# A two-layer hybrid trunk on one core: late mixer steps cut in two on TensorE, with modulation chunks between the pieces

## The reference

```python
mods = (jax.nn.silu(c) @ ada_w + ada_b).reshape(B, 3, 3, 1, D_MODEL)
x = residual(x, 0, _swiglu(modulate(x, 0), ffn_wg[0], ffn_wu[0], ffn_wd[0]), 0.5)
proj = modulate(x, 1) @ w_in
p_rw, p_gla, p_ml = _split(proj, [RW_PROJ, GLA_PROJ, ML_PROJ])
o_rw, ... = _rwkv7_mix(p_rw, ...)      # first mixer
o_gla, ... = _gla_mix(p_gla, ...)      # second: gated linear attention, gates from log_sigmoid(gdown @ a2 + a_b)
o_ml, ... = _mlstm_mix(p_ml, ...)      # third: mLSTM
mix = jnp.concatenate([o_rw, o_gla, o_ml], axis=-1) @ w_out
x = residual(x, 1, mix, 1.0)
x = residual(x, 2, _swiglu(modulate(x, 2), ffn_wg[1], ffn_wu[1], ffn_wd[1]), 0.5)
```

## Time and profile before

| | us |
|---|---|
| device time, median of 3 runs | 1668.06 |
| lowest, highest of them | 1665.26, 1680.5 |
| the profiled execution, its own time | 1668.73 |
| its span, first to last instruction | 1666.6 |

### The profile page before, as it was taken

One profiled execution on the slowest core, in us unless ns is written; L12 is line 12 of the kernel. 1 busy time (PEld: TensorE's weight loads), 2 busy tenths in 40 slices (PEclk: granted clock), 3 DMA queues, 4 the chain that ended last, 5 costly groups with the idle time before them and its releaser, 6 DMA issues. The chain is left out here.

```text
span 1666.6 us, 32873 instructions
## 1 busy us (share of the span) xinstructions
PE 1602.4 (96%) x14052; PEld 1472.9 (88%) x14052; DVE 930.4 (56%) x1593; ACT 672.4 (40%) x997; POOL 203.1 (12%) x271
## 2 busy tenths in 40 slices
PE   5999999999999999999999999999999989899997
PEld 2999999998777779999989999989977768899996
DVE  1544545587663675555474545465865456655544
ACT  2333344564323344333353333355532244543333
POOL 1000011100222330000210000110022242100011
PEclk9999999999997799999999999999999669999998
DMA  8765555443443173444645544734313325344441
GB/s 309 277 220 209 176 213 180 148 123 120 158 160 105 47 277 136 146 149 152 253 165 202 208 168 154 252 123 165 111 61 119 119 79 181 118 148 146 142 161 69
DMA packets 103864, 268.57 MB, mean 161 GB/s; under 512 B 39560, under 2 KB 42024, under 8 KB 103464
## 3 DMA queue, kind: packets, MB, share of 16 engines
q1 hardware_dynamic: 99304, 263.86, 46.1%
q10 hardware_dynamic: 4416, 2.62, 0.6%
HBM read 260.19 MB, written 6.26 MB: 160 GB/s over the span
## 5 line engine op out<-in xcount | busy, mean ns | idle before, releaser
L2408 DVE TENSOR_TENSOR wlo<-raw,whi 128x1024 fp32r<-128x1024 f32 x300 | 367.9, 1229 | 312.7 <-ACT whi L2256 310.0
L2256 ACT ACTIVATE whi<-raw 128x1024 fp32r<-128x1024 f32 x300 | 316.2, 1055 | 290.8 <-PE psV L2067 260.4
L2065 PE MATMUL psA<-XH,whi 128*128 128x320 f32 x1104 | 342.8, 311 | 2.7 <-DVE wlo L2408 2.4
L2066 PE MATMUL psA<-XL,whi 128*128 128x320 f32 x1104 | 341.4, 309 | 0.0
L2067 PE MATMUL psA<-XH,wlo 128*128 128x320 f32 x1104 | 341.3, 309 | 0.0
L2065 PE MATMUL psV<-XH,whi 128*128 128x320 f32 x848 | 266.5, 314 | 0.1
L2066 PE MATMUL psV<-XL,whi 128*128 128x320 f32 x848 | 262.9, 310 | 0.0
L2067 PE MATMUL psV<-XH,wlo 128*128 128x320 f32 x848 | 262.8, 310 | 0.0
L2065 PEld LDWEIGHTS psA<-XH,whi 128*128 128x128 f32 x1104 | 207.7, 188 | 5.1 <-issue 4.1
L2066 PEld LDWEIGHTS psA<-XL,whi 128*128 128x128 f32 x1104 | 207.6, 188 | 0.2
L2065 PE MATMUL psV<-HH,whi 128*128 128x320 f32 x672 | 207.6, 309 | 0.0
(11 more groups left out here) (413 smaller groups left out, 2005.2 us busy)
## 6 DMA issues: line engine op xcount, KB each, us to landing
raw<-weights_dram SPq DMA_DIRECT2D x402, 512.0 KB, 3.3
own<-weights_dram SPq DMA_DIRECT2D x56, 512.0 KB, 5.9
in_xh<-weights_dram SPq DMA_DIRECT2D x6, 512.0 KB, 4.2
in_xl<-weights_dram SPq DMA_DIRECT2D x6, 512.0 KB, 4.5
raw<-weights_dram SPq DMA_DIRECT2D x6, 384.0 KB, 3.6
raw<-weights_dram SPq DMA_DIRECT2D x8, 256.0 KB, 3.6
ZS<-st_rw_dram SPq DMA_DIRECT2D x2, 768.0 KB, 4.4
S<-st_gla_dram ACTq DMA_DIRECT2D x2, 768.0 KB, 4.8
```

Of the source, the lines that this page charges most:

```text
L2065: mm(out, split_hi(n)[:, k], hi[:, kt], start=first, stop=False)
L2066: mm(out, split_hi(n)[:, k], lo[:, kt], start=False, stop=False)
L2256: activation(split_hi(n), buffer(DENSE[n]), ACT.Copy).then_inc(hi_done, 1)
L2408: tt(split_lo(n), buffer(DENSE[n]), split_hi(n).bitcast(F32), ALU.subtract).then_inc(lo_done, 1)
```

## The change

- On PE three generators get one more `yield`: GLA's outputs stop between line 1347 and line 1352; the mLSTM chunk states stop before the product on D1; the mLSTM outputs stop between the two banks. New tokens `gp` and `mp` in `LATE` advance GLA and mLSTM by such a piece, on PE alone.
- `LATE` is written anew: the order of the mixer steps is the old one on every engine, and the chunks stand elsewhere, in layer 0 none before the score steps are over, most of them between the pieces.
- `IN_LATE` of layer 1 is 4, so one of its groups goes to the earlier steps.
- The gates' low product contracts over rows 0 to 111. Rows 0 to 95 of A2G are zero: POOL clears the tile at the start, ahead of MR, and SP's first load of it waits for the mark that both are done.

```diff
 LATE = (
-    ("rw ml ada gl rw ml ada gl ml ada rw gl ml ada rw gl ml ada ada gl ada rw ml ada gl ada rw ml ada gl ada ml ada rw fold "
+    ("rw ml gl rw ml gl ml rw gl ml ada rw gl ml ada mp gl ada gp rw ada ml ada mp ada gl ada gp ada rw ml ada mp ada gl ada ml ada rw fold "
      "gl rw ml su mix rs rw rs su hi.0 rs lo.0 rw hi.1 rw hi.2 lo.1 early.0 rw lo.2 early.1 rw").split(),
-    ("rw ada ml ada gl ada rw ml ada gl ml ada rw gl ada ml ada rw gl ada ml ada gl ada ada rw ada ml ada gl ada ada rw ml ada ada "
-     "gl ada ml ada ada rw fold gl rw ml su mix rs rw rs su hi.0 rs lo.0 rw hi.1 rw hi.2 lo.1 early.0 rw lo.2 early.1 rw").split())
-IN_LATE = (3, 5)
+    ("rw ml gl rw ml gl ml ada rw gl ml ada rw gl ml ada mp ada gl ada gp rw ada ml ada mp ada gl ada gp ada rw ml ada mp ada gl ada ada "
+     "ml ada ada rw fold gl rw ml su mix rs rw rs su hi.0 rs lo.0 rw hi.1 rw hi.2 lo.1 early.0 rw lo.2 early.1 rw").split())
+IN_LATE = (3, 4)
...
-                    bV.close(mm(bank[:, 0:TOK], A2G[DV:DV + 16, j], PJ[DV:DV + 16, T_GR], start=True, stop=True))
+                    bV.close(mm(bank[:, 0:TOK], A2G[0:DV + 16, j], PJ[0:DV + 16, T_GR], start=True, stop=True))
...
                                start=False, stop=False, skip_group_check=True)
+                    yield
                     for s in range(DB):
...
                     bV.close(ins, at("ml_state", c + 2))
+                yield
                 for j in range(MP):
                     bank = bA.open()
                     bA.close(mm(bank[:, 0:TOK], con("pairsel", P, at=j * P), D1_all[:], start=True, stop=True))
...
                     for bank, part in zip(banks, parts):
+                        if part is parts[1]:
+                            yield
...
-                    if L:
-
-                        sp.wait_ge(sem("ml_out"), L)
+                    sp.wait_ge(*((sem("ml_out"), L) if L else (sem("mr_clear"), 1)))
...
+                    elif kind in ("gp", "mp"):
+                        next(mixers[{"gp": "gl", "mp": "ml"}[kind], L])
...
+                G.do(nc.gpsimd.memset(A2G[:], 0.0))
                 G.do(nc.gpsimd.memset(MR[:], 0.0))
                 G.mark(sem("mr_clear"))
```

## The result

The changed kernel took 1677.43 us (median of 6 runs, 1675.71 to 1684.06) beside 1665.37 for the kernel before; ratio 1.0069, 95% interval 1.0035 to 1.0102. A second set of 12 executions, beside other runs of before, gave 1.0029 (1.0009 to 1.0050): 4.8 us between the medians, where the first set had 12.1. It is slower by 0.3 to 0.7%, which is inside the 1% that counts as no change here, but the direction is the same in both sets, and it is not the forecast's: 1663.6 had been predicted, 5.1 us faster. The medians here count every execution, the ratios leave out those more than 1.5% above the fastest of their kernel.

The account below looks back on a forecast made before the run. PE's own order was taken to set the end, slowed by half-clock stretches. Layer 0 -6.9, layer 1 +3.2 and the gates' product -1.4 made -5.1 us against 1668.73: 1663.6, eight in ten between 1650 and 1680.

Parts of the forecast that it names:

- -6.9: Layer 0's late mixer steps: 7.4 us won by less half clock, less 0.5 for a new wait.
- +3.2: Layer 1's late steps: +2.9 for a wait, +1.0 for a piece at half clock, -0.7 won at 1336.4.
- 11.1 us: Layer 0: the most to win if its late half-clock stretches, 3.3 and 23.8 us, all ran at full clock.
- two thirds: Layer 0: share of the possible gain assumed won, 7.4 us, since thin places are fewer but not gone.
- two thin places: Layer 0: RWKV step 4 with GLA and mLSTM chunk states; the 8-column piece with RWKV step 5. The clock may fall there.
- The wait for psA: Layer 0: GLA outputs wait until ScalarE has copied D1 out of two psA banks, 0.5 us.
- Layer 1's wait: Next group's first chunk, behind the first GLA output piece, waits 2.9 us for ScalarE's copy out of psC.
- the upper end: Layer 1's sum at +7.8 us: clock comes back only behind GLA's variance product.
- Gates' product: Layer 0's gates' low product: with 112 more rows its clock fall is expected gone, -1.4 us.
- The wait in front of `su`: PE's wait for VectorE before the state products was to stay near 2.2 us.
- Too thin to bring the clock back: Rival, both layers: single chunks let half clock run until GLA's variance product; +12.4 us, 1681.1; chance 0.17.
- Both layers keep their clock: Rival: late steps of both layers stay at full clock but for a short fall; -20.2 us, 1648.5; chance 0.14.

Follow-up runs that it names:

- l0_new: Changed kernel with layer 1 put back in the old order, so the new order is in layer 0 only: 1667.5 us, ratio 1.0009.
- l1_new: Changed kernel with layer 0 put back in the old order, so the new order is in layer 1 only: 1675.8 us, ratio 1.0042.
- a2g_alone: Changed kernel with the old order in both layers; only the gates' low product over 112 rows and A2G's clearing are left: 1666.0 us, ratio 0.9993.
- wait_old: a2g_alone with two chunks of layer 1 moved so that the old order also has the wait for the copy: 1673.1 us, ratio 1.0028.
- l1_nowait: no_copy_wait with layer 0 in the old order; layer 1 new, without the wait for the copy: 1666.8 us, ratio 0.9994.
- no_copy_wait: Changed kernel with two chunks of layer 1 further forward, so that no chunk waits for the copy: 1668.1 us, ratio 1.0023.
- both_fill: thin_fill2 joined with su_fill2's dense products, and more between RWKV's state products: 1659.7 us, ratio 0.9895.
- thin_fill2: thin_fill with more dense products, and layer 1's last chunk of the fourth late group moved: 1655.6 us, ratio 0.9917.
- thin_fill: no_copy_wait with three dense throwaway products at each of three thin places in each layer: 1661.1 us, ratio 0.9973.
- back_old: l1_new with the old clusters of chunks put back behind layer 1's wait: 1672.1 us, ratio 1.0020.
- su_fill2: a2g_alone with eight dense products in the wait before `su`, in a psA bank, and more between the state steps: 1658.7 us, ratio 0.9930.
- old_fill: Old order with thin_fill's dense products, plus eight before `su` in a psV bank and two at places between the state steps: 1675.4 us, ratio 1.0051.

## Why the prediction was wrong

Two terms of the sum failed, both on where the half clock ends. Layer 0 had -6.9 and gave +1.5; layer 1 had +3.2 and gave +9.8 (l0_new and l1_new against a2g_alone): 8.4 and 6.6 us too low. The sign hung on the first: the prediction itself put the border to "slower" where layer 0 keeps less than 2.3 of its 11.1 us, and it kept none. That 1677.4 lies inside the range of 1650 to 1680 is owed to the width of that range.

*Layer 0: the larger step that failed.* -7.4 was taken ("two thirds"), between ends 0 and 11.1; l0_new against a2g_alone gives +1.5, nothing that can be told from zero. The prediction named two thin places and said that most of the stretch stays if the clock falls at the second. That is what happened: the clock held at the first and fell around the second in every profile of the new order without dense products. Before's short stretch at 496.7 is gone, the long one is not (44.4, 30.7, 23.9, 23.9 us). The "two thirds" stood on no row, and the prediction's own sign of being wrong, that layer 0's stretch stays as long as it was, came true: at the least 23.9 us remain of 27.3. The wait for psA was 0.6 us for 0.5 predicted; whether this new wait has a part in the fall behind it no run tests by itself.

*Layer 1's wait: right.* 2.9 us predicted, 2.6 measured, in the place named, behind the release named. Behind it the clock was expected at half, and there it was in every profile with this wait.

*Layer 1's sum: the other step that failed.* +3.2 was taken, with +7.8 as the upper end, and l1_new against a2g_alone measured +9.8. The prediction let the clock come back near RWKV step 6, because it does so in before. Behind this wait it mostly did not: 47.8 us in three profiles of this order, up to GLA's variance product, the case of the upper end. Worked out by the prediction's own price, 17.1 us more at half (47.8 for 27.3 and 3.4) cost 7.0, with the wait 9.6. The rows of before did not show this length: behind its waits of 2.2 and 2.5 us the clock was back after 23.8. Also missed: the variance product's wait, 1.7 us, because ScalarE's square of the GLA outputs queues behind a copy of MR whose group now closes directly ahead of it; in before the same copy cost 0.5 us there and 0.5 at the chunk in front.

*Gates' product: mechanism right, worth unknown.* No profile with 112 rows has the fall beside layer 0's product; -1.4 fits a2g_alone's ratio, which can't resolve it. In 7 of the 11 profiles with the group moved to layer 1's early steps (after's at 1232.7) a new 3.4 us stretch stands there, in none of the 7 with it in the late ones: the move of a group, priced at nothing, can cost 1.4 (an estimate, 3.4 x 0.41).

*The wait in front of `su`: right,* 2.2 and 2.5 us in all kernels with nothing put into it.

*The rivals.* "Too thin to bring the clock back" gave 1681.1, and the profile of after looks like it, stretches up to the variance product in both layers. But its cause is not what the profiles show for layer 1: the old, clustered order with the wait has the long stretch too (wait_old), the single chunks without it do not (l1_nowait, no_copy_wait). For layer 0 it describes the 44.4 us, which is one outcome of several. "Both layers keep their clock" needed a wait that does no harm, and thin places that are dense enough; both_fill shows what that is worth.

The Trainium skill ("TensorE: Matmul & The Clock Gate", "What's actually happening") sets the clock by how busy the engine has recently been. The runs agree in so far as the clock was at half behind the unfilled waits of 2 us and more, but it fell without one too (no_copy_wait, 1300.2). They do not agree that work alone brings it back: in after PE was busy 45.63 of 47.7 us at half, in thin_fill2 39.17 of 43.0 at full.

**What stays open.** Why layer 0's clock falls at the second thin place, which nine dense products did not prevent in thin_fill's profile (23.9 us). Why the clock stays away longer behind the wait than when it falls without one; wait_old and back_old, which differ in what follows, gave 51 and 34 us, each in one profiled execution. What makes one execution take the earlier place of return and another the later. And what tells both_fill's two executions near 1643 us from its others.

## What to carry to other kernels

Price a wait on the engine that sets the end at its own length and at the half-clock stretch behind it, and give that stretch a wide range: here it lasted 23.8 us behind the waits that before had, and 34 to 51 behind the new one, so that 2.6 us cost 8 to 10. When a gain hangs on whether the clock falls at one place, look for a row that shows that place alone before a share of the gain is put into the sum: the two thirds taken here had none. When a chunk's place in an order written out by hand is moved, follow the copy that frees its bank through the other engine's queue. Where a half-clock stretch is worth 10 us, a few dense products in the wait itself, in a bank that is free by then, won more here (su_fill2, 0.9930) than the new order of the real work; old_fill (1.0051) shows that such products can also lose, so each place has to be measured.

## What the hardware showed unexpectedly

- Work that is thrown away made the program faster: with 25 products of 128 columns in the late and state steps of each layer, and nine in the wait, the fastest of six executions took 1642.5 us, where before's runs beside it had a median of 1667.2; the median of the six was 1659.7.
- TensorE's half-clock stretches differ between executions of one program: 44.4 and 30.7 us in layer 0 of after. The times of l1_new lie in two groups some 9 us apart, with the mean clock to match, so a single profile can show either.
- A wait of 2.6 us was followed by 47.8 us at half clock in all three profiles of that order, with PE busy for over 45 of them; by the times and mean clocks, four of l1_new's 12 executions had some 20 us less at half clock.
